# Where the right-hand weight sum of a seven-product slot is made: an adding transfer issued by GpSimd instead of an addition on VectorE

## The reference, cut to what matters

```python
u = rmsnorm(x, g_mlp) @ w_up
return x + jnp.square(jax.nn.relu(u)) @ w_down      # first MLP
# second MLP
return (jnp.square(jax.nn.relu(x @ w1)) @ w2).astype(x.dtype)
```

## Time and profile before

| | |
|---|---|
| time, median of 3 runs | 2172.2 us |
| the profiled execution's own time | 2172.72 us |
| its span | 2171.0 us |
| TensorE matmul, busy | 2154.7 us (99%) |
| VectorE, busy | 1518.4 us (70%) |
| ScalarE, busy | 1057.6 us (49%) |
| GpSimd, busy | 28.4 us (1%) |
| load queue (hardware_dynamic) | 409.89 MB, 59.2% of 16 engines |
| GpSimd's queue (software_dynamic) | 3.81 MB, 0.6% |

### The profile page before, as it was taken

One profiled execution on the slowest core, in us unless ns is written; L12 is line 12 of the kernel. 1 busy time (PEld: TensorE's weight loads), 2 busy tenths in 40 slices (PEclk: granted clock), 3 DMA queues, 4 the chain that ended last, 5 costly groups with the idle time before them and its releaser, 6 DMA issues.

```text
span 2171.0 us, 28074 instructions
## 1 busy us (share of the span) xinstructions
PE 2154.7 (99%) x11696; PEld 1859.9 (86%) x11696; DVE 1518.4 (70%) x1911; ACT 1057.6 (49%) x1242; POOL 28.4 (1%) x71
## 2 busy tenths in 40 slices
PE   9999999999999999999999999999999999999998
PEld 9988788988888888888898888889888888888886
DVE  6688665566777767698855654546667776667988
ACT  6453564444544444455544444545545443445553
POOL 1000000000000000000001110000000000000000
PEclk9999999999999999999999999999999999999999
DMA  8454445566666666666566654556666666666665
GB/s 259 146 173 159 155 145 179 176 193 194 192 209 196 199 194 194 192 211 195 193 197 202 191 189 158 186 192 193 204 194 195 208 197 196 194 193 194 213 217 190
DMA packets 256414, 415.50 MB, mean 191 GB/s; under 512 B 13284, under 2 KB 167056, under 8 KB 256032
## 3 DMA queue, kind: packets, MB, share of 16 engines
q1 hardware_dynamic: 254800, 409.89, 59.2%
q0 software_dynamic: 1456, 3.81, 0.6%
q10 hardware_dynamic: 32, 0.01, 0.0%
HBM read 409.47 MB, written 4.21 MB: 191 GB/s over the span
## 4 chain that ended last, share of the span: by engine, by line
PE 96%; DVE 3%; ACT 0%; issue 0%; POOL 0%; DVEq 0%; POOLq 0%; ACTq 0%
PE bank L2289 25%; PE bank L2291 12%; PE bank L2419 10%; PE bank L2420 10%; PE bank L2421 10%; PE bank L2262 5%; PE bank L2264 5%; PE bank L2263 5%; PE bank L2302 3%; PE bank L2304 3%; PE bank L2303 3%; DVE wl L1272 1%; PE bank L2535 1%; PE bank L2350 1%; PE bank L2556 0%; PE bank L2565 0%
## 5 line engine op out<-in xcount | busy, mean ns | idle before, releaser
L1272 DVE TENSOR_TENSOR wl<-raw,wh 128x2048 fp32r<-128x2048 f32 x376 | 859.4, 2289 | 251.9 <-ACT wh L718 248.7
L718 ACT ACTIVATE wh<-raw 128x2048 fp32r<-128x2048 f32 x376 | 720.2, 1918 | 427.1 <-DVE raw L1540 203.5
L2289 PE MATMUL bank<-XHL,wh 128*128 128x512 f32 x2368 | 810.8, 390 | 0.0
L2291 PE MATMUL bank<-XHL,wl 128*128 128x256 f32 x2368 | 654.5, 276 | 0.0
L2289 PEld LDWEIGHTS bank<-XHL,wh 128*128 128x128 f32 x2368 | 444.6, 188 | 93.1 <-issue 0.2
L2291 PEld LDWEIGHTS bank<-XHL,wl 128*128 128x128 f32 x2368 | 444.6, 188 | 0.3
L2419 PE MATMUL bank<-wh,hh 128*128 128x512 f32 x792 | 309.1, 390 | 0.0
L2420 PE MATMUL bank<-wl,hh 128*128 128x512 f32 x792 | 308.2, 389 | 0.0
L2421 PE MATMUL bank<-wh,hl 128*128 128x512 f32 x792 | 308.1, 389 | 0.0
L2262 PE MATMUL bank<-wh,XHL 128*128 128x512 f32 x576 | 229.5, 398 | 0.7 <-DVE XHL L1280 0.7
L2264 PE MATMUL bank<-wh,XHL 128*128 128x512 f32 x576 | 224.7, 390 | 0.0
(11 more groups left out here) (452 smaller groups left out, 2022.5 us busy)
## 6 DMA issues: line engine op xcount, KB each, us to landing
raw<-in_mlp_w_dram SPq DMA_DIRECT2D x128, 1024.0 KB, 5.4
raw<-in_w_up_dram SPq DMA_DIRECT2D x64, 1024.0 KB, 5.3
raw<-in_w_down_dram SPq DMA_DIRECT2D x64, 1024.0 KB, 5.5
raw<-in_fox_w_in_dram SPq DMA_DIRECT2D x48, 1024.0 KB, 5.1
raw<-in_w_in_dram SPq DMA_DIRECT2D x40, 1024.0 KB, 4.9
raw<-in_w_out_dram SPq DMA_DIRECT2D x16, 1024.0 KB, 4.9
raw<-in_fox_w_out_dram SPq DMA_DIRECT2D x16, 1024.0 KB, 4.9
raw<-in_w_in_dram SPq DMA_DIRECT2D x16, 256.0 KB, 7.1
```

Source lines behind the costliest of these rows:

```text
L718: act.activation(slot(wh, b, j), slot(raw, b, j), ACT.Copy).then_inc(hi_ready, 1)
L1272: dve.tensor_tensor(slot(wl, b, j), slot(raw, b, j), slot(wh, b, j).bitcast(F32), ALU.subtract)\
L2289: pe.matmul(bk[:, :].rearrange("p (s t) -> p s t", s=2), sh, XHL[:, k, :, :], start=k == 0, stop=False, skip_group_check=True)
L2291: mm = pe.matmul(bk[:, 0:TOK], sl, XH[:, k, :], start=False, stop=k == KT - 1, skip_group_check=True)
```

## The change

VectorE's addition in place goes. In its stead GpSimd, for each unit in the order of use, waits until the slot has landed and issues a transfer from DRAM that adds: its source is w22 read again from the weight matrix (128 x 512 float32, 256 KB), its destination the slot's second block in `raw`, its operation add. `mixed_right` becomes four semaphores, one for each place of the ring, since transfers that are in flight together can't be told apart on one; `right_added` counts how many transfers of that place have to have landed (16 for each). ScalarE and VectorE wait for that count. The 23 transfers of the first MLP stand in GpSimd's program behind the load of `GS`, those of the second at its end.

```diff
--- before.py
+++ after.py
@@ -259,7 +259,7 @@
         comb_sums = sem("comb_sums")
         comb_high = sem("comb_high")
         comb_low = sem("comb_low")
-        mixed_right = sem("mixed_right")
+        mixed_right = [sem(f"mixed_right{i}") for i in range(4)]
         mixed_part = sem("mixed_part")
         mixed_sums = sem("mixed_sums")
         mixed_high = sem("mixed_high")
@@ -439,6 +439,12 @@
 
             return SECOND if half and c else UNITS[half]
 
+        def right_added(m, half, c, s):
+
+            before = [z for mm in (1, 3) for h in range(2) for cc in range(2) for z in units(h, cc)
+                      if (mm, h, cc, z) <= (m, half, c, s) and z % 4 == s % 4]
+            return 16 * len(before)
+
         def parts(m, half, c):
 
             return PARTS * (m // 3) + 11 * half + 6 * c
@@ -673,6 +679,20 @@
             wait_full(pool, ("diag", 1, 1))
             pool.dma_start(GS[:, :], g_ssd[0].unsqueeze(0).broadcast_to([P, SSD_W])).then_inc(gs_landed, 16)
 
+            def right_sums(w_b, b0):
+
+                for half in range(2):
+                    for c in range(2):
+                        b = b0 + half * B_HALF + UP + 4 * c
+                        for s in units(half, c):
+                            j, r = s % 4, half * HALF + 2 * P * s + P
+                            pool.wait_ge(raw_landed[j], landed(b + s // 4, j))
+                            pool.dma_start(slot(raw, b + s // 4, j)[:, 1, :],
+                                           w_b[r:r + P, PAIR * c + 512:PAIR * c + PAIR], accum_op=ALU.add)\
+                                .then_inc(mixed_right[j], 16)
+
+            right_sums(w_down[0], B_M1)
+
             pool.wait_ge(chunk_used, 4 * B_FOX)
             pool.memset(Uf[:, :], 1.0).then_inc(pool_order, 1)
             pool.memset(ONE[:, :], 1.0).then_inc(pool_order, 1)
@@ -701,6 +721,8 @@
                                                  fill=NEG, base=0, pattern=[[-1, P]], channel_multiplier=1)
                     ins.then_inc(bias_ready, 1)
 
+            right_sums(mlp_w2[0], B_M2)
+
 
         @block.scalar
         def _(act):
@@ -827,7 +849,7 @@
                     if s in units(half, c):
                         i = UNITS[half].index(s)
                         n = mixed_unit(m, half, c, i)
-                        act.wait_ge(mixed_right, n + 1)
+                        act.wait_ge(mixed_right[s % 4], right_added(m, half, c, s))
                         hi(b + s // 4, s % 4)
                         act.wait_ge(mixed_sums, n + 1)
                         if half:
@@ -1537,8 +1559,7 @@
                     dve.wait_ge(raw_landed[j], landed(b + s // 4, j))
                     dve.wait_ge(chunk_used, after_slot(b, UNITS[half][i - back]) if i >= back else 4 * b)
                     (t0, _, _), (t1, _, _), (t2, _, _) = mixes(m, half, i)
-                    dve.tensor_tensor(w[1], w[1], w[3], ALU.add).then_inc(mixed_right, 1)
-                    dve.wait_ge(mixed_right, n + 1)
+                    dve.wait_ge(mixed_right[j], right_added(m, half, c, s))
                     dve.tensor_tensor(t1, w[0], w[1], ALU.add).then_inc(mixed_part, 1)
                     dve.wait_ge(mixed_part, n + 1)
                     dve.tensor_tensor(t0, t1, w[3], ALU.subtract)
```

## The result

The changed kernel takes 2226.65 us (median of four executions, 2224.61 to 2229.56), the kernel before 2172.2 beside it: ratio 1.0252, interval 1.0239 to 1.0265. The profiled execution took 2224.84 us, its span is 2223.0: 52.0 us more than the span before.

What follows compares the result with a forecast made beforehand. TensorE, busy 99% of the span, was taken as the bound. Gain 0 and a loss of 4 x 2.4 = 9.6 us in half 1 raised the median from 2172.2 to 2181.8 us; range 2171.3 to 2212.

Steps and rivals of the forecast that it cites:

- The bound and the gain: TensorE has hardly a wait to take away; removing VectorE's 46 additions, 31.6 us, gains between 0 and 0.9 us, taken as 0.
- A: Time from a unit slot's landing to that of its sum by the adding transfer; between 3.4 and 8.3 us, taken as 5.5.
- d: Delay of the next slot's load landing because the adding transfer's bytes take room; one to two times 0.82 us, taken as 1.2.
- the addition's own read: An addition in place reads the slot's 256 KB as well; 0.82 us more if the reads do not overlap.
- Single slots: Units not side by side, as in half 0: no loss with A up to 5.5 us; slot 11 only up to 4.9.
- the rule: A slot is in time if A + 4.4 us is no more than the distance from its landing to TensorE's need.
- Half 1: With side-by-side units, each pass loses 1.8 us at slot 6 and 0.6 at slot 11; four passes, 9.6 us.
- just in time: Half 1's slots 8 and 9 get 1.8 us more from the pause at slot 6, so they lose nothing.
- Behind the new waits: What queues behind the new waits on ScalarE, VectorE and GpSimd adds no term; SP gains no wait.
- Hidden: Rival: A below 4.8 us makes the loss at half 1's slot 6 under 4.3 us, so not slower; chance 0.32.
- GpSimd held up by VectorE: Rival: each transfer's issue is held 2.1 us, A is 7.6, loss 51.6 us in both halves, 2224 us; chance 0.08.
- A slow addition: Rival: reading, adding and writing do not overlap; A of 8.3 gives 2239 us, A of 7 gives 2212; chance 0.15.

Runs made afterwards that it cites:

- copy: Against the changed kernel, the transfer copies instead of adding, and the sum with w12 is left out; 2203.48 us, ratio 1.0144.
- GpSimd adds late: Against the kernel where GpSimd adds in SBUF without a transfer, the addition waits until the next slot's load has landed; 2219.39 us, ratio 1.0218.
- quarter: Against the changed kernel, the transfer adds 128 of the 512 columns, 64 KB, and the other columns' sum is left out; 2193.13 us, ratio 1.0098.
- turned round: Against the changed kernel, SP holds the load behind a unit only until GpSimd has issued its adding transfer; 2236.73 us, ratio 1.0296.
- the held load: Against the changed kernel, SP issues the load behind a unit only when the unit's adding transfer has landed; 2299.39 us, ratio 1.0584.
- four multiplications: Against the kernel where GpSimd adds in SBUF, four in-place multiplications by 1.0 stand ahead of each addition; 2321.21 us, ratio 1.0686.

## Why the prediction was wrong

**The bound and the gain: right.** TensorE without a gap, VectorE's 31.6 us worth nothing: the kernel with GpSimd's addition in SBUF takes the same 46 additions from VectorE, 13.6 us of its busy time on balance, and measures 1.0006.

**The size of A: wrong, and this is the step that failed.** "Nearest in size and surroundings is 5.2 ... I take 5.5." Measured 7.25. The 5.2 was a median of four transfers whose place in time against the loads I had not looked at. A unit's transfer nearly always meets the same one: TensorE paces the loads at 5.44 or 4.77 us and they land after about 5.5, so the landing that lets GpSimd go is nearly the moment at which SP sends the next megabyte. I saw this (2012.44 against 2012.5) and charged it to the load, as d, and not to the transfer that comes behind it. The price is 4.2 us alone (4.48 from the slot's landing) and 7.0 in line. The term for the addition's own read was near: 0.82 us reckoned, 1.0 measured between copy and addition.

The Trainium skill's page "DMA: Bandwidth & Descriptors", section "Queues, rings and completion order", says that a DMA engine takes turns between queues by whole packets, of 9 to 17 descriptors typically. In this trace the records of a load are of 4.1 KB (0.88 MB in 216), so a 1 MB load is some 16 for each of 16 engines, about one such packet. If that is the packet of the rule, it would have foretold what the rows show, a transfer that waits for nearly the whole load ahead of it; which records form a packet, no run here shows.

**d: too high.** 1.2 was taken; loads behind a unit land 0.57 us later (median), 6.05 after their issue and not 6.7. Most of the transfer runs after the load, not beside it. Between slots 5 and 6, the pair for which the term was written, the second landing even came 0.2 to 1.5 us nearer to the first.

**Single slots: in sum the rule held, with the right A.** "One over 6.7 brings half 0 in": three of five units of a half-0 pass at A - 5.5 make 3 x 1.75 = 5.25 us; measured 5.1 (mean of four). The loss isn't spread as the rule has it: slots 3, 6, 8, 11 and 13 lose 1.2, 1.0, 0.6, 1.5 and 0.4 us, not three of them 1.75. Three other kernels in which the next load isn't held come within 0.7 us:

| kernel | A | half-0 pass: 3 x (A - 5.5) | measured | half-1 pass, rule | measured |
|---|---|---|---|---|---|
| changed | 7.25 | 5.3 | 5.1 | 5.3 | 8.0 |
| GpSimd adds late | 6.88 | 4.1 | 4.0 | 4.2 | 7.4 |
| copy | 6.21 | 2.1 | 2.8 | 2.9 | 5.5 |
| quarter | 5.90 | 1.2 | 1.2 | 2.3 | 4.5 |

**Half 1: a second, smaller error.** The rule counted slot 6 (A + d - 4.9; d is 0.57, 0.2, 0.3, 0.31 in these kernels, like A a median of all units) and slot 11 (A - 4.9), and is 2 to 3 us a pass too low. In the changed kernel the loss is spread over the units and the slots behind pairs: slot 3 1.27 us, 5 0.55, 6 1.68, 7 0.53, 8 0.72, 9 1.14, 11 1.42, 13 0.35 (means of the four passes). Slot 7's share is nearly all clock, the 1.6 us of the one stretch at the lower level; the other three kernels have one such stretch each in half 1 too, 0.4 us a pass. Slots 8 and 9, which I had called "just in time", lose, and so does slot 3, a single slot to which I gave no term in half 1: in the kernel before TensorE wanted it 10.5 to 10.8 us after its landing, so by the same reckoning (4.4 us after the sum) it is late from an A of 6.1 to 6.4 on. With A = 7.25 and d = 0.57 my working would have given 4 x 5.25 + 4 x 5.3 = 42 us, 2214; the other 11 of the 52.7 are this. How a pause passes from one unit to the next I have not worked out further.

**Behind the new waits:** that none of them adds a term was right. GpSimd issues 0.28 us after the landing.

**The rivals.** *Hidden* was refuted by the landing. *GpSimd held up by VectorE* came nearest in number (A = 7.6: 2224), but not in cause: the issues take 850 to 931 ns, and in the unit shown VectorE stands idle for 5.24 of the 7 us. *A slow addition* has the measured A between its two cases (A = 7: 2212; 8.3: 2239), but an addition costs only 1.0 us more than a copy. The chance of slower (0.68) was on the right side; the range ended at 2212, since A over 6.7 had 0.15 and the held GpSimd 0.08.

**Not tried:** a smaller load ahead of the transfer, or pairs of units taken apart, either of which would give the transfer room. No kernel here beats the one before; in the waits for `wl` there were 0.9 us to win.

## What to carry to other kernels

A transfer's duration from another place of the trace holds only for that place's traffic: look what will stand ahead of it in the DMA engines at the moment when its wait is released, and add that. If an event lets both a large load and a small urgent transfer go, the small one pays for the large one; turning the order makes the load pay. An addition that costs a busy engine 0.69 us, inside its slack, is cheaper than one that costs this engine nothing and is there 7 us later, when the work behind it can wait 5.5. And a wait of TensorE can cost more than itself: read the granted clock of the stretch behind it.

## What the runs showed of the hardware

- A 256 KB transfer that adds from DRAM into SBUF takes 4.2 us alone: first data packet after 1.57, the packets 2.3. GpSimd's instruction takes 0.86 us, for a copy 0.54.
- Behind a 1 MB load it takes 7.0, a copy 6.0, 64 KB 5.6. Between two queues the larger part of the earlier transfer went ahead of the later one, in both orders: where the load was issued first, 87% of its packets had begun before the transfer's first (median); turned round, 72% of the transfer's before the load's first.
- With some of TensorE's waits (2.0 to 5.6 us long) a stretch at a granted clock of 0.50 (1.2 of 2.4 GHz) began, with matmuls 0.43 us apart instead of 0.227: 1.6 us lost in the changed kernel, 18 with the held load, 42 with four multiplications.
- GpSimd's addition of 128 x 512 float32 takes 1.32 us in the median, 3.43 at most while VectorE works, against 0.69 on VectorE. The Trainium skill's page "SBUF — State Buffer", section "SBUF: two separate sides", has the two share ports under an exclusive lock; the stretched instructions of both engines agree.
